# Two transformer blocks on one core: another step table for the first attention stage

## The reference, cut to what matters

```
h    = rmsnorm(x, norm1_g) * (1 + sc1) + sh1
proj = h @ w_in                        # q (512), k (128), v (128), u_pool (512)
att  = blocked_gqa(rope(norm(q)), rope(norm(k)), v)   # 8 query heads, 2 kv heads
pool = pool_mixer(u_pool)              # 4 groups of 128: centred mean over 2, 4, 8, 16
                                       # tokens minus self, then a 128x128 product each
mix  = concat([att, pool]) @ w_out
x    = x + g1 * mix
h2   = rmsnorm(x, norm2_g) * (1 + sc2) + sh2          # then the FFN, then block 2
```

## Time and profile before

| | |
|---|---|
| median of 3 runs | 1400.04 us (1399.88 to 1403.12) |
| profiled execution | 1400.04 us |
| its span in the trace | 1398.2 us |
| PE busy | 1352.8 us (97%) |
| DVE, POOL, ACT busy | 764.1, 704.0, 635.3 us |

### The profile page before, as it was taken

One profiled execution on the slowest core, in us unless ns is written; L12 is line 12 of the kernel. 1 busy time (PEld: TensorE's weight loads), 2 busy tenths in 40 slices (PEclk: granted clock), 3 DMA queues, 4 the chain that ended last, 5 costly groups with the idle time before them and its releaser, 6 DMA issues.

```text
span 1398.2 us, 17598 instructions
## 1 busy us (share of the span) xinstructions
PE 1352.8 (97%) x7007; PEld 1114.5 (80%) x7007; DVE 764.1 (55%) x1249; ACT 635.3 (45%) x1174; POOL 704.0 (50%) x382
## 2 busy tenths in 40 slices
PE   6889799999999999999999999999999999999998
PEld 6666489888888888897777777778888888888886
DVE  5579935777676574556776755325185421312224
ACT  5446645444331431645777755564554332313321
POOL 1248752656663564555333554448607654645560
PEclk8899999999999999999999999999999999999999
DMA  8324641555555553411121221124302222222321
GB/s 333 146 89 137 204 151 61 202 194 189 199 180 210 194 183 130 142 61 62 60 91 61 64 88 61 47 74 151 120 1 86 96 90 90 91 94 93 114 92 60
DMA packets 32050, 167.54 MB, mean 120 GB/s; under 512 B 3552, under 2 KB 4192, under 8 KB 18912
## 3 DMA queue, kind: packets, MB, share of 16 engines
q1 hardware_dynamic: 31968, 166.42, 34.5%
HBM read 164.31 MB, written 2.10 MB: 119 GB/s over the span
## 4 chain that ended last, share of the span: by engine, by line
PE 85%; DVE 7%; ACT 3%; POOL 2%; issue 1%; DMA 1%; SPq 0%; DVEq 0%; ACTq 0%
PE B L552 82%; PE B L972 1%; DVE ZF L1873 1%; POOL WL L2302 1%; ACT WH L1193 1%; DVE SC L1787 1%; DVE ZF L1864 1%; DVE ST L1973 1%; DMA SC<-in_w_ada 1%; DVE SC L1956 0%; DVE SC L1951 0%; POOL HL L2314 0%; PE B L796 0%; DVE XT L2010 0%; DMA ZF<-in_w_ada_rows 0%
## 5 line engine op out<-in xcount | busy, mean ns | idle before, releaser
L2302 POOL TENSOR_TENSOR WL<-RAW,WH 128x512 fp32r<-128x512 f32 (+1 forms) x203 | 471.2, 2336 | 467.2 <-ACT WH L1193 421.9
L552 PE MATMUL B<-HH,WH 128*128 128x512 f32 (+2 forms) x1040 | 403.9, 391 | 4.0 <-ACT HH L1275 2.1
L552 PE MATMUL B<-HH,WL 128*128 128x512 f32 (+2 forms) x1040 | 396.6, 384 | 0.0
L552 PE MATMUL B<-HL,WH 128*128 128x512 f32 (+2 forms) x1040 | 385.4, 382 | 0.0
L1193 ACT ACTIVATE WH<-RAW 128x512 fp32r<-128x512 f32 (+1 forms) x203 | 192.9, 980 | 194.7 <-PE B L552 178.2
L552 PEld LDWEIGHTS B<-HH,WH 128*128 128x128 f32 x1040 | 196.3, 189 | 44.9 <-issue 5.7
L552 PEld LDWEIGHTS B<-HH,WL 128*128 128x128 f32 x1040 | 196.2, 189 | 38.8
L552 PEld LDWEIGHTS B<-HL,WH 128*128 128x128 f32 x1040 | 191.4, 188 | 34.5
L552 PE MATMUL B<-ZR,WH 128*128 128x512 f32 (+1 forms) x624 | 164.8, 353 | 0.7 <-POOL WL L2302 0.7
L2314 POOL TENSOR_TENSOR ZR<-SC,ZR 128x512 fp32r<-128x512 f32 (+1 forms) x72 | 96.9, 1348 | 117.2 <-ACT ZR L1687 50.8
L1873 DVE CUSTOM_DVE_ANT_0 ZF<-ZF,VT 128x1024 f32<-128x1024 f32 x80 | 135.7, 1722 | 11.1 <-DMA ZF<-in_w_ada_rows 11.0
(11 more groups left out here) (254 smaller groups left out, 1773.3 us busy)
## 6 DMA issues: line engine op xcount, KB each, us to landing
RAW<-in_slabs SPq DMA_DIRECT2D x102, 1024.0 KB, 4.9
ZF<-in_w_ada_rows SPq DMA_DIRECT2D x80, 512.0 KB, 4.3
G<-in_w_ada SPq DMA_DIRECT2D x8, 512.0 KB, 10.5
RAW<-in_slabs SPq DMA_DIRECT2D x4, 768.0 KB, 4.5
RAW<-in_x SPq DMA_DIRECT2D x4, 512.0 KB, 6.3
SC<-in_w_ada SPq DMA_DIRECT2D x4, 512.0 KB, 9.2
ZF<-in_w_ada SPq DMA_DIRECT2D x4, 512.0 KB, 9.9
out<-SC SPq DMA_DIRECT2D x8, 256.0 KB, 2.1
```

The source lines that it names most:

```text
L552: return e.matmul(out, l, r, start=start, stop=stop)
L2302: e.tensor_tensor(lo[:, at], k.RAW[:, i % 2, at], hi[:, at].bitcast(F32), ALU.subtract).then_inc(*w.hit((i, q)))
```

## The change

It gives four of the step tables other numbers. Nothing is added or left out: 24 modulation tiles, 20 projection steps, four pool products and four first halves of output tiles stand in the loop before and after.

```diff
-ADA1 = [*range(5, 16, 2), *range(16, 31), 32, 34, 36]
+ADA1 = [*range(9, 20, 2), *range(20, 38)]
 
-T1 = {"q3": 0, "p0": 5, "p1": 10, "p2": 15, "p3": 20}
+T1 = {"q3": 0, "p0": 4, "p1": 9, "p2": 13, "p3": 18}
 
-POOL_OUT = {24: 0, 25: 1, 26: 2, 28: 3}
+POOL_OUT = {22: 0, 23: 1, 24: 2, 26: 3}
 
-MIX = {30: 0, 31: 1, 33: 2, 34: 3}
+MIX = {28: 0, 29: 1, 32: 2, 34: 3}
```

## The result

The changed kernel takes 1408.73 us (median of 6 runs, 1407.53 to 1409.92), the kernel before 1400.22 us (6 runs, 1399.88 to 1403.12). The ratio is 1.0055, with a 95% interval of 1.0042 to 1.0068: 0.55% slower, 8.5 us. The forecast was 1400.7 us in a range of 1396.4 to 1403.8, so the time lies above the range.

What follows compares the result with a forecast made beforehand. PE, busy 97%, bounds the kernel, with 13.1 us of idle time to win. The 3.4 us gained on PE are given back as stalls for a late ol3, plus 0.6: 1400.04 + 0.6 = 1400.7 us, range 1396.4 to 1403.8.

Steps and rivals of the forecast that it cites:

- The bound, and the early steps: PE bounds, 13.1 us idle at most to win; early, the L1752 wait shrinks from 2.0 to 0.8, unit 5 starts at 108.8.
- the two projection steps that PE was ahead: Steps 10 to 21: PE's lead of two projection steps brings DVE's maxima of unit 10 only 0.4 us sooner.
- One of its signs: Sign that the forecast is right: up to 140 us, PE's waits for L1752 and for exponentials get smaller.
- Steps 20 to 30: DVE full at 6.0 us a unit; PE idles some 4 us before group 3's product; unit 15's maxima start at 171.5.
- now it hangs on unit 11: 149.9: POOL's low part of group 0 follows unit 11's exponentials, 4.64 us after its maxima, and starts at 149.9.
- the mean ends at 159.5: POOL takes 9.6 us from group 0's low part to the end of group 3's mean; PE's product starts at 159.7.
- Attention terms 3.4 us ahead: Steps 30 to 35: PE reaches the output tiles' attention terms at 183.8 instead of 187.22, the gain on PE.
- The loop's end: Steps 32 to 38: five load-bound tiles ahead of L1993, 15.3 us after tile 30; L1993 at 191.6, ol3 ends at 194.3.
- the rule of 193.7: At the loop's end, an ol3 later than 193.7 costs PE one us per us; at 194.3 PE is 0.6 us late.
- Rival 2: Tail costs more: loads of 4.5 us in tiles 32 to 36, 1402.7; with unit 15 1.5 later, 1404.2; chance 0.20.
- Behind that all is as before: same tiles, same norm chain, same loads: Behind the first half tiles, after the late ol3, nothing changes, so no further time is added.

Runs made afterwards that it cites:

- e6: Changed kernel with the product of pool group 3 back in step 28 and the output tiles in their old steps: 1404.45 us, ratio 1.0021.
- e9: Kernel before with ten unread maxima (6.03 us) on DVE ahead of the last L1993, so that ol3 comes late: 1406.44 us, ratio 1.0039.
- e4: Changed kernel without the loads of the tiles of steps 32 to 36, multiplying what lies in the buffers: 1404.08 us, ratio 1.0020.
- e7: Kernel before with only a new tile list, early steps and 16, 33, 35 free of tiles: 1398.59 us, ratio 0.9982.
- e8: Changed kernel with group 3's product and output tiles in their old steps, and a tile list leaving steps 33 and 35 free: 1402.56 us, ratio 1.0009.
- e10: Kernel before with the tile list of e7 and the first two output tiles a step later, in 31 and 32: 1398.29 us, ratio 0.9976.
- e2: Changed kernel with the old tile steps, so projections, pool products and output tiles moved alone: 1408.19 us, ratio 1.0046.
- e2 again: Changed kernel with the old tile steps, run once more unchanged for a second profile: 1409.43 us in one run.
- e11: Kernel before with two unread maxima (1.2 us) on DVE in step 7, lengthening PE's wait for L1752: 1403.15 us, ratio 1.0008.
- e3: Changed kernel with seven unread matmuls on PE ahead of the products of pool groups 2 and 3: 1407.04 us, ratio 1.0034.
- e5: Changed kernel with the old tile steps and unread matmuls ahead of the products of pool groups 2 and 3: 1407.46 us, ratio 1.0042.

## Why the prediction was wrong, step by step

**The bound, and the early steps: right.** Unit 5 began at 29.8 us after unit 0, as the 108.8 of the prediction says; the wait for L1752 came out at 0.72 (0.8 taken), and unit 5 waited for exponentials, 2.38 us, as said. Unit 10 came 1.0 us later than worked out (60.3 against 59.3), for the gaps before units 7 and 9 are 0.76 and 0.49, not 0.25 in all. Unit 12 was where it had been: the two projection steps that PE was ahead bought nothing. DVE sets the pace there, as the prediction said. One of its signs was wrong: up to unit 10 the waits for exponentials did not shrink, they grew from 3.0 to 3.8 us.

**Steps 20 to 30: the step that failed first.** It is the start of the low part of group 0, "now it hangs on unit 11: 149.9", and with it "the mean ends at 159.5": I hung the pool chain on ACT alone. ACT had the rounded half of group 0 ready at 151.44 (150.3 on the clock of before, 149.9 predicted), but POOL did not stand free: ol1 had come to it only at 148.88, for its rounded part stands in ACT's queue behind two copies of a projection (the earlier p3 put them there), and behind ol1 two windows took 4.10 us. The low part started at 154.18, or 153.0 on the clock of before, 3.1 us late. From there to the end of the mean POOL took 8.4 us and not 9.6, which made up 1.2. The product of group 3 so began at 162.74, or 161.6 on the clock of before, and not at 159.7: 1.9 us. The wait that I had put at some 4 us there was split in two, 2.64 before unit 13 and 2.93 before the product.

**The clock: a term that wasn't in the sum.** From the product to unit 14 I took 3.4 us and it was 5.1. The product took 1.76 us instead of 1.10 and the product with v 2.92 instead of 1.95, 1.6 us together, and the stretches there show why:

```profile
156.00:158.00 2.00, 1.67 (x7) 0.93 (x8) 2.00 (x5) 1.97 (x6) 1.92 (x2) 0.55 0.21 84
158.00:160.00 2.00, 1.81 (x8) 1.48 (x8) 2.00 (x3) 1.12 (x3) 2.00 (x2) 0.60 0.68 168
...
164.00:166.00 2.00, 2.00 (x9) 0.99 (x10) 1.29 (x2) 1.32 (x2) 0.83 (x2) 0.50 0.51 133
```

Behind each of the two waits the chip granted little more than the lower of the clock's two levels (0.55 and 0.60, then 0.50, that is 1.2 of 2.4 GHz). The sum treated PE's idle time as free to be moved about; here the work behind two of its waits ran slow. The length of a wait alone doesn't tell when. Before, PE waited as long ahead of unit 14, and the clock stayed at 1.00 from 150.5 to 167 us:

```profile
162.61 0.96 PE L552 MATMUL B<-ZR 64*128 64x512 f32 x6 [2.94 <-ACT SC L1351]
```

Both together, 1.9 and 1.7, are the 3.6 us by which units 14 and 15 are later than worked out (u15 at 95.1 against 91.5). e6 shows that they hang on the places of product and output tiles: with both back, unit 14 is 5.0 us earlier and unit 15 6.9.

**Attention terms 3.4 us ahead: wrong, without cost.** P came 2.0 us late instead of 3.4 early. Besides the 3.6, PE waited 1.5 us for POOL's split of an output tile (WL L2302) that I had without a gap. None of it counts, for ol3 was later still.

**The loop's end: the mechanism right.** From unit 15's maxima to the end of tile 30 it took 4.15 us (4.77 taken), from there to L1993 16.2 (15.3), and ol3 ended 2.72 after L1993's start, as before. All five tiles ahead of L1993 waited for their loads. On the clock of before, ol3 ended at 198.2 and not at 194.3: the 3.9 us are the 3.6 of unit 15 and 0.3 of the loop. By the rule of 193.7 that is a loss of 4.5 us; M is 4.7 us late. That the two agree so well is luck in part. In e9 M began 3.8 us after the end of ol3, here 4.8, because POOL's first quarter of out2 took 2.29 us and not 1.29 beside DVE's tile of step 37 (198.19 above), which wasn't in the sum; without this 1.0 us the rule would be too high, as it was in e9 by 0.7. e4 shows the late ol3 from the other side, e9 by itself. Rival 2 had this place and this rule, and put the price on slower loads. The three loads that DVE waited for (issued at 180.44, 185.93 and 190.93) took 4.14, 3.66 and 4.46 us, 12.3 in all; that is more than the sum had taken and less than the rival's 13.5, and makes the 0.9 us between 16.2 and 15.3. The larger part of its lateness came from unit 15, and its far end was 1404.2.

Of the two rules of the Trainium skill, that of "SBUF — State Buffer", section "Who interferes with whom" (two-input DVE instructions and GpSimd ones that read SBUF shut each other out), agrees with the trace: the tile at 180.33 beside POOL's split took 2.27 us, the five behind it, with POOL idle, 1.28 each; tile 30 ended 0.6 us sooner behind the maxima than in the sum, where I had allowed up to 1.3. By the other, in "DMA: Bandwidth & Descriptors", section "Anatomy of one DMA", I had estimated 3.2 us for a load. That section gives its fit for DMAs that GpSimd issues, and these are issued by SP, so the estimate was taken from another path; the shortest load in the earlier trace rows took 3.4. Here 5.65 us lie between the end of the tile at 186.42 and the start of the one at 193.35 that uses its buffer anew, with a 1 MB slab in the same queue from 186.30.

**"Behind that all is as before: same tiles, same norm chain, same loads": wrong, 1.5 us.** From M to N it took 15.1 us, 13.6 before. Two things hang on the late ol3 there. The first is a slab. It is issued when the last quarter of out2 has been split: at 205.33 (195.96 before), 8.2 us later counted from unit 0, which is 7.2 by ol3 and 1.0 by the quarter of 2.29 us. It also took 6.18 us to land, not 5.04, and why isn't known. Before, it landed at 201.00, 3.1 us ahead of ACT's copy; now ACT waited 0.79 us for it, until 211.53; the squares of the norm stand behind these copies, DVE's sums wait for the squares, and PE waits for the sums (L1771) before N. The second is the other 0.7 us, which passed before ACT came to the slab. The copies of the slab start 7.4 us behind M, 5.9 before, and only 0.79 of the difference is a wait. POOL's splits of out2 and out3 now last until 7.1 us behind M, 3.2 before, and DVE's sums, which have two inputs in SBUF, run beside them and are longer. The second of these sums, before and after:

```profile
201.60 0.69 DVE L1771 TENSOR_TENSOR SC<-SC 128x512 f32<-128x512 f32 x1 [0.70 <-ACT SC L1206]
```
```profile
207.21 1.59 DVE L1771 TENSOR_TENSOR SC<-SC 128x512 f32<-128x512 f32 x1 [0.70 <-ACT SC L1206]
```

e9 shows the same two, 0.66 us of waiting in its 1.4 and sums of 1.61 us. In e7, e8 and e10 ACT waits for no slab, POOL's splits last until 4.5 to 5.0 us behind M, and M to N still takes 0.9, 1.2 and 1.4 us longer than before, which is, to 0.1 us, what the first two sums take longer in each. No run has one without the other in the changed kernel, so the split into 0.8 and 0.7 is read from the trace and not timed. I had priced what a late ol3 does to PE and not what it does to the queue of loads and, by POOL, to DVE.

**The sum.** Predicted +0.6; 3.9 by the later ol3; 0.8 by the slab and 0.7 by DVE's slower sums; 0.2 unaccounted: the 6.2 us up to N. The ratios of the medians are 1.0046 for the tables without the tiles, 0.9991 for the tiles without the tables, 1.0055 for both; 1.0021 with the product back in step 28 and the output tiles with it, 1.0020 without the late loads. The halves don't add up: alone the tiles cost nothing, and beside the tables their profiles show 2.3 us won up to P and 4.3 lost from P to N (after against e2).

**What stays open.** The medians differ by 8.5 us, the profiles by 6.7 without the start. In 71 runs of the kernel before, a mean clock lower by 0.001 goes with 0.7 us; the changed kernel's runs have 0.983 to 0.986, that before mostly 0.986 to 0.989, so the clock can carry 1 to 2 us of it. This is a relation between runs and not an experiment: no run sets the clock to one value. What decides whether an execution's clock falls behind a given wait isn't settled either.

## What to carry to other kernels

Time of an engine off the bound isn't free where it sits: behind waits of PE of 2 to 5 us the work ran at a lowered clock in some executions, which a single profile may or may not show, and moving steps moves these waits. When a step is moved, follow every queue it leaves a copy in (here ACT's, ahead of a rounding that POOL wanted), and when a product comes late, follow also the loads that its consumers release, and what the work behind it will now run beside. Where a change has two halves, time them apart: here one was harmless and pointed to a version 0.24% faster than the kernel before (0.14 to 0.33%).

## What the runs showed of the chip

- Behind waits of PE of 2 to 3 us the granted clock fell to about half for some us in some executions and not in others. The same wait of 2.97 us (e2 and e2 again) was followed by a product with v of 1.95 and of 3.68 us; the same of 2.05 us (before and e9) by 1.95 and 2.93. The Trainium skill ("TensorE: Matmul & The Clock Gate", "HAM oscillation — how this bites in real kernels") describes falls of the clock behind PE's waits for DMA. Here they stood behind waits for other engines, and the same wait was followed by one in one execution and not in the other. One fall cost 1.1 us at P (e9) and 2.7 and 2.8 us at unit 5 (e2 again, e11).
- A wait lengthened by 1.2 us cost 4.0 us at unit 5 where the clock fell with it (e11). In the median of ten runs it was 1.4 us, with an interval that reaches to no difference.
- Filling the waits with matmuls kept the clock at 1.00 and won 0.7 us at unit 15 of the 1.7 that its fall had cost (e3), and in e5 nothing that its ratio shows; in e3 the filling also made unit 13 1.9 us later.
- DVE's sum of two 128x512 tensors in SBUF took 0.69 us with POOL idle and 1.6 us beside POOL's splits (before and after, L1771); a quarter of a split on POOL took 1.29 us and, where DVE's tile of 2.24 us had begun first, 2.29.
- The first matmul of the attention scores began between 78.8 and 81.0 us in the profiled executions, 2.1 us apart for one and the same kernel.
